# One kernel, its second mixer rewritten: projection in three parts, attention among the slabs, a new recurrent pipeline

## The chip, the cores and the metric

The program runs on one core of one Trainium2 chip. The metric is the device time of one execution in microseconds (us), so lower is better. A run of the kernel before takes 3675.67 us (median of three, 3661.73 to 3676.49). About 0.5% is what a measurement of this kernel can tell from no change.

## What is computed

Two transformer-like blocks of depth 2 follow each other over 512 positions of width 1024, all in float32. The change touches one mixer: the second layer of the first block. Cut to what matters there:

```python
h  = rms_norm(x, mix_norm[1])
p  = h @ w_in                                  # 1024 -> 2560 = 1024 (xb) + 1024 (gate) + 512 (mq)
xb, gate, mq = split(p, [1024, 2048])
xc = centred_depthwise_conv(xb, conv_w, conv_b)         # 4 taps along the positions
y  = rg_lru(xc, ..., False) + rg_lru(xc, ..., True)     # forward and backward
y  = y * gelu(gate)
mo = memory_attention(mq, mk, mv)              # 4 heads of 128, 256 memory rows, softmax
x  = x + concat([y, mo]) @ w_out[1]            # 1536 -> 1024
# rg_lru, for each block n of 128 channels (8 of them):
r = sigmoid(xc_n @ wa_n + ba);  i = sigmoid(xc_n @ wx_n + bx)
log_a = -8 * r * softplus(-lam);  a = exp(log_a)
u = sqrt(-expm1(2 * log_a)) * (i * xc_n);  h_t = a_t * h_(t-1) + u_t
```

## The kernel before

Activations are held transposed: 128 features on the partitions, 512 positions along the row, so a 1024-wide tensor is eight tiles of 128x512. A dense product reads its weights as *slabs* of 16 blocks of 128x128 (1 MB): SP loads a slab into `w_raw`, ScalarE (ACT) rounds it to `w_hi`, VectorE (DVE) makes the rest `w_lo`, and TensorE (PE) adds three products, hi·hi, hi·lo and lo·hi, per block (`TERMS`). Each of the three buffers holds two slabs, number s in half s % 2; the split of slab s+2 therefore waits until PE has finished slab s. `PHASES` lists the dense products in program order, and every engine walks through that list in its own instruction stream. Each stream is in order and is held up by semaphore waits that are written out by hand. There is no scheduler.

The second mixer is four stages, one after the other:

1. `in1_1` (`product`, PE line 764; `scaled`, DVE line 1367): ten slabs, each gives two tiles of `proj`. PE streams and the other engines split weights and evict.
2. `attention(SECTIONS["mem1"])`: four units of 128 positions. PE makes the scores (line 828), DVE copies and takes the maximum (1491, 1493), ACT the exponentials (1124), PE transposes (837), ACT copies (1138), PE weighs the values (847), DVE divides (1522), PE transposes back (859), DVE splits into `mixM_hi` and `mixM_lo` (1551, 1553).
3. `gates` (`lru_gates` on PE, `lru` on ACT and DVE, `gelu_arguments` on POOL): eight tiles. For each one DVE makes the convolution (1650), ACT and DVE its hi and lo parts (1167, 1662), PE four products in three terms each (907), ACT tanh and exp of them (1178, 1183, 1188, 1192), DVE the decays (1671 to 1678), ACT a square root (1197), DVE the two scans and the output (1686 to 1694), ACT and DVE `mixL_hi` and `mixL_lo` (1214, 1712).
4. `out1_1` (`product` again): eight slabs of 12 blocks, one output tile each. It starts with this wait, so all eight recurrent tiles come first:

```python
elif p.layer == 1:
    pe.wait_ge(y_ready, DT)
```

The activation tables of ACT have to be loaded anew between tanh or exp and the square root (`ACT_TABLE_LOAD`).

## Time and profile before

| | us |
|---|---|
| median of three runs | 3675.67 |
| the profiled execution, its own time | 3670.74 |
| its span, first to last instruction | 3668.9 |
| outside of the span | 1.8 |
| PE busy | 3364.1 (92%) |
| DVE busy | 1849.5 (50%) |
| ACT busy | 1120.0 (31%) |
| POOL busy | 460.1 (13%) |

PE is the busiest engine. Its matmuls are pipelined and overlap in the record, so a busy PE may still be slower than it could be. The span has three regions where PE is clearly less busy. The first of them is the second mixer, between 745.7 us and 1098.8 us; the rest of the program isn't touched by the change.

### The profile page before, as it was taken

What the parts mean: (1) busy time and instruction counts of PE and PEld (TensorE: products, weight loads), DVE (VectorE), ACT (ScalarE), POOL (GpSimd) and SP (SyncE); (2) the same over time, 40 slices, a digit from 0 to 9 for tenths busy, and PEclk for the clock granted to TensorE, in tenths of its full rate; (3) what the DMA queues carried; (4) which work ended last, traced back from release to release, by engine and by line L of the source; (5) the groups of instructions that cost most, each with busy time, mean ns of one, the idle gap of its engine ahead of it and who ended that gap; (6) DMA issues with size and microseconds to landing.
All of it is one profiled execution on the core that took longest, in us unless ns stands there. A gap on an engine that the chain in (4) does not pass through costs nothing.

```text
span 3668.9 us, 41039 instructions
## 1 busy us (share of the span) xinstructions
PE 3364.1 (92%) x15236; PEld 2759.4 (75%) x15236; DVE 1849.5 (50%) x1904; ACT 1120.0 (31%) x1267; POOL 460.1 (13%) x426
## 2 busy tenths in 40 slices
PE   8898999997379999999997689999999997689998
PEld 6687888885268887888885668888888885668886
DVE  5665534434955254544535654445444535654444
ACT  3243322223732122322314323223322314323221
POOL 1000100100120006000202620002000202620002
PEclk9899999998589999999997689999999997589999
DMA  3111222221022222422220012223322320012222
GB/s 139 53 47 49 100 103 92 100 95 40 9 77 92 103 92 97 115 93 97 98 101 35 1 37 101 91 99 104 108 102 87 107 92 35 1 44 94 92 99 73
DMA packets 46038, 292.98 MB, mean 80 GB/s; under 512 B 5408, under 2 KB 5920, under 8 KB 18432
## 3 DMA queue, kind: packets, MB, share of 16 engines
q1 hardware_dynamic: 44496, 287.04, 22.3%
q0 software_dynamic: 1456, 4.79, 0.8%
q8 instruction: 55, 0.90, 0.1%
q14 instruction: 31, 0.25, 0.0%
HBM read 289.70 MB, written 2.10 MB: 80 GB/s over the span
## 4 chain that ended last, share of the span: by engine, by line
PE 84%; DVE 9%; POOL 3%; ACT 2%; issue 2%; DMA 0%; DVEq 0%; SPq 0%; POOLq 0%; ACTq 0%
PE ps L764 76%; POOL dec L695 2%; PE ps L847 2%; PE ps L828 1%; PE ps L837 1%; DVE gfin L1806 1%; PE ps L796 1%; DVE mx L1493 1%; DVE xc L1650 1%; PE ps L807 1%; PE ps L966 1%; DVE w_lo L1319 0%; DVE sc_n L1488 0%; PE ps L859 0%; DVE tmp L1531 0%
## 5 line engine op out<-in xcount | busy, mean ns | idle before, releaser
L764 PE MATMUL ps<-xg_hi,w_hi 128*128 128x512 f32 x2592 | 1014.3, 391 | 17.6 <-DVE w_lo L1319 17.6
L764 PE MATMUL ps<-xg_lo,w_hi 128*128 128x512 f32 x2592 | 1009.5, 389 | 0.0
L764 PE MATMUL ps<-xg_hi,w_lo 128*128 128x512 f32 x2592 | 1009.2, 389 | 0.0
L1319 DVE TENSOR_TENSOR w_lo<-w_raw,w_hi 128x2048 fp32r<-128x2048 f32 (+1 forms) x292 | 681.6, 2334 | 280.0 <-ACT w_hi L1031 279.9
L1031 ACT ACTIVATE w_hi<-w_raw 128x2048 fp32r<-128x2048 f32 (+1 forms) x292 | 552.0, 1890 | 701.8 <-PE ps L764 701.8
L764 PEld LDWEIGHTS ps<-xg_hi,w_hi 128*128 128x128 f32 x2592 | 487.2, 188 | 121.6 <-issue 20.2
L764 PEld LDWEIGHTS ps<-xg_lo,w_hi 128*128 128x128 f32 x2592 | 487.2, 188 | 103.5 <-issue 2.7
L764 PEld LDWEIGHTS ps<-xg_hi,w_lo 128*128 128x128 f32 x2592 | 487.2, 188 | 101.2
L764 PE MATMUL ps<-hid_hi,w_hi 128*128 128x512 f32 x1216 | 473.4, 389 | 0.0
L764 PE MATMUL ps<-hid_lo,w_hi 128*128 128x512 f32 x1216 | 473.0, 389 | 0.0
L764 PE MATMUL ps<-hid_hi,w_lo 128*128 128x512 f32 x1216 | 473.0, 389 | 0.0
L1406 DVE SCALAR_TENSOR_TENSOR x<-ps,x 128x512 f32 (+1 forms) x128 | 88.6, 692 | 432.1 <-PE ps L764 432.1
L1394 DVE TENSOR_TENSOR tmp<-ps,r_bc 128x512 f32<-128x512 f32 x176 | 121.7, 692 | 323.2 <-PE ps L764 307.9
L764 PEld LDWEIGHTS ps<-hid_hi,w_hi 128*128 128x128 f32 x1216 | 228.2, 188 | 48.8 <-issue 1.4
L764 PEld LDWEIGHTS ps<-hid_hi,w_lo 128*128 128x128 f32 x1216 | 228.2, 188 | 47.5
L764 PEld LDWEIGHTS ps<-hid_lo,w_hi 128*128 128x128 f32 x1216 | 228.2, 188 | 47.0
L574 POOL TENSOR_TENSOR ssq<-x 128x512 f32<-128x512 f32 x9 | 9.3, 1038 | 1919.4 <-DVE x L1406 1919.4
L1084 ACT ACTIVATE xg_hi<-x,vec x72 | 52.1, 724 | 403.0 <-DVE x L1406 403.0
L1074 ACT ACTIVATE hid_hi<-tmp 128x512 f32 x88 | 55.7, 633 | 387.9 <-DVE tmp L1397 387.9
L1367 DVE TENSOR_TENSOR proj<-ps,r_bc 128x512 f32 (+1 forms) x76 | 52.5, 691 | 201.3 <-PE ps L764 200.9
L1072 ACT ACTIVATE tmp<-tmp 128x512 f32<-128x512 f32 x88 | 55.6, 632 | 269.0 <-DVE tmp L1394 269.0
L953 PE MATMUL ps<-fac 64*128 64x128 f32 (+1 forms) x576 | 82.6, 409 | 39.1 <-DVE fac L1755 38.0
(281 smaller groups left out, 3410.7 us busy)
## 6 DMA issues: line engine op xcount, KB each, us to landing
w_raw<-up_dram SPq DMA_DIRECT2D x120, 1024.0 KB, 4.7
w_raw<-in_dram SPq DMA_DIRECT2D x42, 1024.0 KB, 4.8
w_raw<-down_dram SPq DMA_DIRECT2D x32, 1024.0 KB, 4.7
w_raw<-down_dram SPq DMA_DIRECT2D x32, 768.0 KB, 4.2
w_raw<-down_dram SPq DMA_DIRECT2D x32, 640.0 KB, 3.9
w_raw<-out_dram SPq DMA_DIRECT2D x16, 768.0 KB, 4.2
w_raw<-out_dram SPq DMA_DIRECT2D x8, 1024.0 KB, 4.7
w_raw<-memk_dram SPq DMA_DIRECT2D x4, 1024.0 KB, 4.7
```

Of the source, the lines that this page charges most:

```text
L695: last = pool.tensor_tensor(to[:, :, u, :], (half, mid)[1 - u], (mid, half)[1 - u], ALU.subtract)
L764: last = pe.matmul(ps[:, 2 * q + b, :], (w_hi, w_lo)[wp][:, q, t:t + P], parts[xp], start=(k == 0 and m == 0), stop=(k == p.ktiles - 1 and ...
L847: last = pe.matmul(ps[:, u.o_bank, i * u.d:(i + 1) * u.d], turned(u)[:, kb, i * P:(i + 1) * P], u.v[kb][i], start=(kb == 0), stop=(kb == u ...
L953: last = pe.matmul(ps[:, 4 * (j % 2) + hd, c0:c0 + w], keys[:, s0:s0 + P], queries[:, t0:t0 + w], start=True, stop=True)
L1031: act.activation(w_hi[:, q, 0:w], w_raw[:, q, 0:w], ACT.Copy).then_inc(hi_done, 1)
L1072: act.activation(tmp[:, 0, :], tmp[:, 0, :], ACT.Silu).then_inc(silu_done, 1)
L1074: act.activation(pick(hid_hi, j), tmp[:, 1, :], ACT.Copy).then_inc(hid_h, 1)
L1084: act.activation(pick(xg_hi, m), pick(x, m), ACT.Copy, scale=g).then_inc(xg_h, 1)
L1319: dve.tensor_tensor(w_lo[:, q, 0:w], w_raw[:, q, 0:w], w_hi[:, q, 0:w].bitcast(F32), ALU.subtract)\
L1367: dve.tensor_tensor(pick(proj, j), ps[:, 2 * q + b, :], r_bc[:], ALU.mult)\
L1394: dve.tensor_tensor(tmp[:, b, :], ps[:, 2 * q + b, :], r_bc[:], ALU.mult).then_inc(evac, Q // 2)
L1406: dve.scalar_tensor_tensor(out=pick(x, m), in0=ps[:, 2 * q + b, :], scalar=p.alpha, in1=pick(x, m), op0=ALU.mult, op1=ALU.add).then_inc(ev ...
```

## The change

The projection is three phases now: `in1_1q` (memory queries, 2 slabs), `in1_1x` (recurrent input, 4), `in1_1g` (gate, 4). `out1_1` is six slabs of 16 blocks: for each half of the output (four tiles) one slab for the memory part and two for the recurrent part. From `in1_1x` on, each engine runs one hand-written sequence, `mixer()` (on POOL `lru()`). In the kernel's numbering, "inner" is an input slab and "outer" a gate slab. The gate weights of the recurrence are no longer split: they are loaded as float32 (`wg_lru`) and each product is one float32 matmul in place of three. Some steps of a tile move from DVE to POOL (squares of the decays, the sum of the two scans, the last factors of the gelu), and the root is taken on `l_t`. Buffers are laid out anew, so that `xg_hi` and `xg_lo` stay alive during the mixer.

```diff
@@ plan
+            ph.append(Phase("in1_1q", "proj", 2, 16, 2, norm=norm, layer=1, tile0=16))
+            ph.append(Phase("in1_1x", "mixer", 4, 16, 2, norm=norm, layer=1, tile0=0))
+            ph.append(Phase("in1_1g", "mixer", 4, 16, 2, norm=norm, layer=1, tile0=8))
+            ph.append(Phase("out1_1", "mixer", 6, 16, 4, alpha=1.0, last=True, next_norm=norm + 1, layer=1))
@@ SP
+            if p.name == "in1_1x":
+                sp.wait_ge(o_psum, SECTIONS["window"][-1].n + 1)
+                sp.dma_start(wg_lru[0][:], a["gates"][0]).then_inc(wg_in[0], 16)
+            if p.name == "out1_1":
+                sp.wait_ge(o_psum, M1[-1].n + 1)
+                sp.dma_start(wg_lru[1][:], a["gates"][1]).then_inc(wg_in[1], 16)
@@ POOL, lru()
+            def decay_squares(n):
+                if n:
+                    pool.wait_ge(sqrt_in, n)
+                pool.wait_ge(te_e, 2 * (n + 1))
+                pool.tensor_tensor(l_w[:], l_e[:, n % 2], l_e[:, n % 2], ALU.mult).then_inc(a2_done, 1)
...
+            for n in range(DT):
+                if n + 1 < DT:
+                    gelu_argument(n + 1)
+                state_sum(n)
+                if n + 1 < DT:
+                    decay_squares(n + 1)
+                    gelu_gate(n + 1)
@@ PE, mixer()
+            def gates(n):
+                pe.wait_ge(wg_in[n // 4], 16)
+                pe.wait_ge(conv_done, n + 1)
...
+                    pe.wait_ge(gate_read, n)
                 for g in range(4):
                     t = ((n % 4) * 4 + g) * P
+                    last = pe.matmul(ps[:, 4 + g, :], wg_lru[n // 4][:, t:t + P], xc[:, n % 3, :], start=True, stop=True)
+            def out(h, part):
+                s = MIX_O + 3 * h + part
+                pe.wait_ge(lo_done, s + 1)
+                if part == 0:
+                    pe.wait_ge(evac, EV0 + Q * (MIX_O + 3 * h))
+                for b in range(4):
+                    for k in range(4):
+                        if part and not (h or b):
+                            pe.wait_ge(y_ready, 4 * (part - 1) + k + 1)
...
+            inner(0)
+            scores(M1[0]); scores(M1[1])
+            inner(1)
+            turn_probs(M1[0]); scores(M1[2]); weigh(M1[0]); turn_probs(M1[1]); scores(M1[3]); turn_out(M1[0])
+            inner(2)
+            weigh(M1[1]); turn_probs(M1[2]); turn_out(M1[1]); weigh(M1[2]); turn_probs(M1[3]); turn_out(M1[2]); weigh(M1[3])
+            inner(3)
+            turn_out(M1[3])
+            outer(0); gates(0); outer(1); gates(1); outer(2); gates(2); outer(3); gates(3)
+            out(0, 0); gates(4); gates(5); out(0, 1); gates(6); gates(7); out(0, 2)
+            out(1, 0); out(1, 1); out(1, 2)
@@ ACT, mixer()
+            splits = {0: MIX_G + 3, 1: MIX_O, 2: MIX_O + 1, 3: MIX_O + 2, 5: MIX_O + 3}
             for n in range(DT):
+                if n in splits:
+                    split(splits[n])
+                if n + 3 < DT:
+                    first_tap(n + 3)
                 if n + 1 < DT:
                     gates(n + 1)
+                    root(n + 1)
+                high(n)
@@ DVE, mixer()
+            front(M1[0], 0); front(M1[1], 1); inner(0); split(MIX_X + 2); conv(0); inner(1); split(MIX_X + 3)
+            front(M1[2], 2); back(M1[0]); front(M1[3], 3); finish(M1[0]); inner(2); back(M1[1]); split(MIX_G); conv(1)
+            back(M1[2]); finish(M1[1]); finish(M1[2]); back(M1[3]); conv(2); inner(3); split(MIX_G + 1); finish(M1[3])
+            outer(0); split(MIX_G + 2); inputs(0); decays(0)
...
+            def decays(n):
+                dve.wait_ge(a2_done, n + 1)
+                dve.wait_ge(te_done, n + 1)
+                dve.scalar_tensor_tensor(out=l_t[:, n % 2], in0=l_w[:], scalar=1.0, in1=l_t[:, n % 2], op0=ALU.add,
+                                         op1=ALU.mult).then_inc(sqrt_in, 1)
...
+            for n in range(DT):
+                recur(n)
+                if n < 3:
+                    outer(n + 1)
+                if n in splits:
+                    split(splits[n])
+                if n + 1 < DT:
+                    inputs(n + 1)
+                    decays(n + 1)
+                output(n)
+                if n + 3 < DT:
+                    conv(n + 3)
+                low(n)
+            split(MIX_O + 4)
+            for b in range(4):
+                add(0, b)
```

(Statements that stand on lines of their own in the source are joined with ";" in the lists of PE and DVE.)

The order of the instructions shows it at two places. First ACT, from the last slab of the projection to the first recurrent tile (`sc` or `sc_m` are the scores, `pt` or `pt_m` the turned ones, `xc` the first tap of the convolution, `w_hi` a slab's split, `l_t` the gate). Before:

```order
L1031 ACTIVATE w_hi<-w_raw 128x2048
L1053 REGISTER_ALU
L1053 COMPARE_AND_BRANCH
L1124 ACT_TABLE_LOAD
L1124 ACTIVATE sc,rowsum<-sc,nmx 128x256 x8
L1138 ACTIVATE pt<-ps 128x1024
L1124 ACTIVATE sc,rowsum<-sc,nmx 128x256 x4
L1138 ACTIVATE pt<-ps 128x1024
L1124 ACTIVATE sc,rowsum<-sc,nmx 128x256 x4
L1138 ACTIVATE pt<-ps 128x1024 x2
```

And in the changed kernel:

```order
L1264 ACTIVATE sc_m,rowsum<-sc_m,nmx 128x256 x8
L1309 ACTIVATE xc<-proj,vec 128x512 x2
L1275 ACTIVATE pt_m<-ps 128x1024
L1172 ACTIVATE w_hi<-w_raw 128x2048
L1264 ACTIVATE sc_m,rowsum<-sc_m,nmx 128x256 x4
L1275 ACTIVATE pt_m<-ps 128x1024
L1172 ACTIVATE w_hi<-w_raw 128x2048
L1264 ACTIVATE sc_m,rowsum<-sc_m,nmx 128x256 x4
L1275 ACTIVATE pt_m<-ps 128x1024 x2
L1309 ACTIVATE xc<-proj,vec 128x512
L1172 ACTIVATE w_hi<-w_raw 128x2048 x2
```

Weight splits now stand between the steps of the attention. Second DVE, one tile of the recurrence, from one output to the next. Before:

```order
L1694 SCALAR_TENSOR_TENSOR l_y<-l_y,tmp 128x512
L1662 TENSOR_TENSOR xc_lo<-xc,xc_hi 128x512
L1671 SCALAR_TENSOR_TENSOR l_v<-l_v,xc 128x512 x2
L1675 SCALAR_TENSOR_TENSOR l_e<-l_e,l_t 128x1024
L1677 TENSOR_SCALAR l_a<-l_e 128x1024
L1678 SCALAR_TENSOR_TENSOR l_w<-l_a,l_e 128x1024
L1712 TENSOR_TENSOR mixL_lo<-l_y,mixL_hi 128x512
L1650 SCALAR_TENSOR_TENSOR xc<-proj,vec,xc 128x511 x2
L1650 SCALAR_TENSOR_TENSOR xc<-proj,vec,xc 128x510
```

And in the changed kernel:

```order
L1870 SCALAR_TENSOR_TENSOR l_y<-l_y,l_v 128x512
L1832 SCALAR_TENSOR_TENSOR xc<-proj,vec,xc 128x511 x2
L1832 SCALAR_TENSOR_TENSOR xc<-proj,vec,xc 128x510
L1875 TENSOR_TENSOR mixL_lo<-l_y,mixL_hi 128x512
L1861 TENSOR_TENSOR l_v<-l_v,l_t 128x1024
L1862 SCALAR_TENSOR_TENSOR l_v<-l_e,l_v 128x512
L1863 SCALAR_TENSOR_TENSOR l_v<-l_e,l_v 128x512
L1817 TENSOR_TENSOR proj<-ps,r_bc 128x512 x2
L1486 TENSOR_TENSOR w_lo<-w_raw,w_hi 128x2048
L1845 SCALAR_TENSOR_TENSOR l_v<-l_v,xc 128x1024
L1853 SCALAR_TENSOR_TENSOR l_t<-l_w,l_t 128x1024
```

The tile has fewer vector steps of its own, and the evictions of a gate slab and the split of a weight slab stand in the middle of it.

## Rows read from the trace of the kernel before

**Rows 1.** The page, part 2: PE busy tenths in 40 slices of the span.
```profile
PE   8898999997379999999997689999999997689998
```
**Rows 2.** Windows, four stages: stretch, length, busy PE, PEld, DVE, ACT, POOL; PEclk, DMA.
```profile
745.70:856.40 110.70, 109.82 (x483) 90.24 (x481) 41.66 (x33) 21.31 (x13) 2.70 (x2) 1.00 0.26 93
856.40:891.70 35.30, 24.57 (x144) 20.52 (x144) 21.14 (x29) 15.80 (x40) 7.86 (x6) 0.87 0.07 23
891.70:1030.30 138.60, 39.56 (x96) 28.38 (x96) 115.67 (x130) 91.61 (x119) 20.39 (x18) 0.60 0.02 6
1030.30:1098.80 68.50, 68.45 (x290) 56.43 (x291) 28.62 (x23) 18.01 (x15) 17.28 (x13) 0.96 0.27 93
```
**Rows 3.** Waits from 856 to 1031 us: us in total, times, longest.
```profile
PE ps L907 <- DVE xc_lo L1662: 76.9, 7, 13.2
...
PE ps L764 <- DVE mixL_lo L1712: 20.9, 1, 20.9
```
**Rows 4.** Timeline, DVE: start, us, engine line op; second evictions of two neighbouring slabs.
```profile
757.77 0.69 DVE L1367 TENSOR_TENSOR proj<-ps,r_bc 128x512 f32 x1 [0.51 <-PE ps L764]
...
768.64 0.69 DVE L1367 TENSOR_TENSOR proj<-ps,r_bc 128x512 f32 x1 [4.75 <-PE ps L764]
```
**Rows 5.** Timeline, PE, in the attention.
```profile
869.70 2.05 PE L847 MATMUL ps<-mv,pt 128*128 128x128 f32 x16 [0.16 <-ACT pt L1138]
871.58 1.04 PE L837 MATMUL ps<-ident,sc 128*128 128x128 f32 x8
872.46 1.89 PE L828 MATMUL ps<-mk,proj 128*128 128x256 f32 x8
```
**Rows 6.** Timeline, PE: four float32 products 128x512, two records for each.
```profile
2134.35 3.60 PE L966 MATMUL ps<-att,vtok_g 128*128 128x512 f32 x8
```
**Rows 7.** Timeline, DVE: a split; a convolution twice; a 128x1024 step; a scan.
```profile
857.50 2.29 DVE L1319 TENSOR_TENSOR w_lo<-w_raw,w_hi 128x2048 fp32r<-128x2048 f32 x1 [1.13 <-ACT w_hi L1031]
...
913.39 2.32 DVE L1650 SCALAR_TENSOR_TENSOR xc<-proj,vec,xc 128x511 f32<-128x511 f32 x3 [1.83 <-ACT xc L1160]
...
928.25 3.51 DVE L1650 SCALAR_TENSOR_TENSOR xc<-proj,vec,xc 128x511 f32<-128x511 f32 x3 [1.31 <-ACT xc L1160]
931.68 1.22 DVE L1686 SCALAR_TENSOR_TENSOR l_v<-l_v,l_w 128x1024 f32<-128x1024 f32 x1
932.93 1.22 DVE L1687 TENSOR_TENSOR_SCAN l_h<-l_a,l_v 128x512 f32<-128x512 f32 x1
```
**Rows 8.** Timeline, ACT: one tile of the recurrence, from root to root.
```profile
942.41 1.06 ACT L1197 ACTIVATE l_w<-l_w 128x1024 f32<-128x1024 f32 x1 [3.12 <-DVE l_w L1678]
943.38 0.80 ACT L1160 ACTIVATE xc<-proj,vec 128x512 f32<-128x512 f32 x1
944.19 1.28 ACT L1178 ACT_TABLE_LOAD   x1
945.49 0.69 ACT L1178 ACTIVATE l_t<-ps,hb 128x512 f32<-128x512 f32 x1
...
947.94 1.52 ACT L1183 ACTIVATE l_e<-l_t,lam_s 128x512 f32<-128x512 f32 x2
...
950.92 0.61 ACT L1192 ACTIVATE l_y<-l_y 128x512 f32<-128x512 f32 x1
...
958.45 1.06 ACT L1197 ACTIVATE l_w<-l_w 128x1024 f32<-128x1024 f32 x1 [3.12 <-DVE l_w L1678]
```
**Rows 9.** Timeline, POOL: the three gelu steps of one tile.
```profile
927.03 1.04 POOL L669 TENSOR_TENSOR l_y<-proj 128x512 f32<-128x512 f32 x1 [62.35 <-DVE mixL_lo L1712]
928.15 0.62 POOL L671 TENSOR_SCALAR l_y<-l_y 128x512 f32<-128x512 f32 x1
928.85 1.57 POOL L673 TENSOR_TENSOR l_y<-l_y,proj 128x512 f32<-128x512 f32 x1
```
**Rows 10.** Timeline, PE: start of the output product, and its first matmul at full rate.
```profile
1030.35 0.79 PE L764 MATMUL ps<-mixL_hi,w_hi 128*128 128x512 f32 x1 [20.92 <-DVE mixL_lo L1712]
...
1036.03 0.39 PE L764 MATMUL ps<-mixL_lo,w_hi 128*128 128x512 f32 x1
```

More of the change, by code:

```diff
@@ L780, in product @@
                 first = 2
-            with pe.Fori(first, p.slabs // 2) as i:
-                slab(i, 0)
-                slab(i, 1)
+            if first < p.slabs // 2:
+                with pe.Fori(first, p.slabs // 2) as i:
+                    slab(i, 0)
+                    slab(i, 1)
         def memory_slab(n):
@@ new lines, in scores @@
+        def scores(u):
+            if u.n:
+                pe.wait_ge(s_read, u.n)
+            if u.kind == "memory" and u.layer == 0:
+                pe.wait_ge(evac, EV0 + Q * (MEM_SLAB + MEM_SLABS))
+            for i in range(4):
+                for bank, col, off, n in score_pieces(u, i):
+                    o, keys = ps[:, bank, col:col + n], u.k[i]
+                    if u.kind == "near":
+                        o = o.rearrange("p (r c) -> p r c", c=SLAB_C)
+                    else:
+                        keys = keys[:, off:off + n]
+                    last = pe.matmul(o, u.q[i], keys, start=True, stop=True)
+            last.then_inc(s_ready, 1)
@@ new lines, in turn_out @@
+        def turn_out(u):
+            if u.kind == "near":
+                pe.wait_ge(on_ready, u.nf + 1)
+            else:
+                pe.wait_ge(o_ready, u.n + 1)
+            if u.f:
+                pe.wait_ge(ot_ready, u.f)
+            for t in range(u.ntile):
+                last = pe.transpose(ps[:, u.ot_bank, u.ot_col + t * P:u.ot_col + (t + 1) * P],
+                                    tmp[:, u.f % 2, t * P:(t + 1) * P], ident[:])
+            last.then_inc(ot_psum, 1)
+        def attention(us):
@@ L990, in _ @@
                     attention(SECTIONS["window"])
[L991 to L994 removed]
+                elif p.layer >= 2:
                     l = p.layer - 2
@@ L1001, in _ @@
                     gla(l)
-            elif p.kind == "gates":
-                lru_gates(p)
+            elif p.kind == "mixer":
+                if p.name == "in1_1x":
+                    mixer()
             elif p.kind == "resid" and p.src == "mix":
@@ L1220, in gla_prep @@
+            for b in range(4):
+                next_high(1, b)
+            split(MIX_END + 1)
         def gla_prep(p, l):
@@ L1286, in _ @@
                 rms(p.norm)
-            if p.kind == "gates":
-                lru(p, p.next_tiles * P)
+            if p.kind == "mixer":
+                if p.name == "in1_1x":
+                    mixer()
                 continue
@@ new lines, in mixer @@
+            inner(3)
+            split(MIX_G + 1)
+            finish(M1[3])
+            outer(0)
+            split(MIX_G + 2)
+            inputs(0)
+            decays(0)
+            splits = {0: MIX_G + 3, 1: MIX_O, 2: MIX_O + 1, 3: MIX_O + 2, 5: MIX_O + 3}
+            for n in range(DT):
[11 more added lines that the diff above has]
+                low(n)
@@ L1718, in gla_prep @@
+            split(MIX_O + 4)
+            for b in range(4):
+                add(0, b)
+                if b:
+                    next_low(0, b - 1)
+            next_low(0, 3)
+            split(MIX_O + 5)
+            split(MIX_END)
+            for b in range(4):
+                add(1, b)
+                if b:
+                    next_low(1, b - 1)
+            next_low(1, 3)
+            split(MIX_END + 1)
         def gla_prep(l):
@@ L1843, in _ @@
                 rms(p.norm)
-            if p.kind == "gates":
-                lru(p, p.next_tiles * P)
+            if p.kind == "mixer":
+                if p.name == "in1_1x":
+                    mixer()
                 continue
```

627 lines of the change are left out of this document (357 added, 270 removed).

## The prediction, made before the changed kernel ran

> **What bounds the kernel now.** I read PE's row by slices first. Among digits of 8 and 9 stands 7, 3, 7 for the tenth to twelfth slice [rows 1]. The windows of the four stages come next [rows 2]. In the projection (110.7 us) and the output product (68.5 us) PE is busy all the time. In the attention (35.3 us) it is busy for 24.6, and in the recurrence (138.6 us) for 39.6, while DVE is busy for 115.7 of these. So two stages of 174 us belong to DVE, ACT and their hand-overs, and PE waits. The waits say the same: the gate products waited 76.9 us for `xc_lo`, the output product 20.9 us for the last `mixL_lo` [rows 3]. The whole mixer takes 353.1 us. Only this part can change; the rest of the program has the same instructions.
>
> **What the change moves.** I write the time from the start of the first query slab, 745.7 us, as t = 0. The mixer ends at t = 353.1 now. I follow each engine's new order with the durations of the rows.
>
> PE alone. A slab of 48 matmuls takes 10.9 us (768.64 - 757.77) [rows 4]. One attention unit takes about 1.9 for the scores, 0.9 for the turn and 1.9 for the values (starts 869.70, 871.58, 872.46) and some 0.5 to turn the output, so 5.2, four of them 20.8 [rows 5]. The gate product of a tile was 12 matmuls, a quarter of a slab's, so 2.7 us at full rate; now it is four float32 products. Four of these took 3.6 us [rows 6], so I take 3.5 with the overlap off: eight tiles cost 28 us instead of 22. The output product has 288 blocks' matmuls before and after (8 slabs of 12 blocks, 6 of 16), six slabs of 10.9. Together 10 x 10.9 + 1 + 20.8 + 28 + 65.2 = 224 us. Below that the mixer can't go.
>
> Part A, queries and inputs with the attention. Six slabs (65.2), the norm's sum (1), attention (20.8). The waits that remain for PE, each read from the orders: second scores behind the copy of the first, 1.3 (a 128x1024 step is 1.22 [rows 7]); fourth scores behind DVE's split, 1.9 (a split is 2.29 [rows 7]); two turns and one value product behind a split and a convolution on ACT and DVE, 0.4 + 1.7 + 2.7. Sum 8. Part A ends at t = 95. Splits hide behind PE's slabs, as they do in the projection now [rows 2].
>
> Part B, gate slabs with tiles 0 to 3. PE needs 10.9 + 3.5 per tile, so it could be through at 95 + 58 = 153. DVE can't follow. Its steps between the decays of one tile and of the next are: output and `mixL_lo`, 0.7 each; convolution, 2.3; product with the root and two scans, 3 x 1.22; inputs and decays, 2 x 1.25; two evictions, 1.4; one split, 2.3. Sum 13.5 [rows 4, 7]. On top comes POOL. While POOL's gelu steps run, the convolution takes 3.51 instead of 2.32 [rows 7, 9]. The POOL work beside it is about 0.5 of the short step and 1.26 to 1.57 of the last one, say 1.7 to 2.1, so DVE loses 0.6 to 0.7 us per us of POOL. POOL now has per tile the same three steps (2.9), a step of 128x1024 (twice 1.04), one more short step (0.6) and two more of 1.3 [rows 9], 8.2 us instead of 3. The square falls where DVE waits for it, so 6.1 of them meet DVE: 0.7 x 6.1 = 4.3. Period: 13.5 + 4.3 = 17.8.
> ACT's period, for comparison: tap and table load 2.1, from the first tanh to the end of the gelu's tanh 6.0, load 1.3, root 1.1, high part 0.6, split 1.9, thus 13 us [rows 8]. It waits for DVE, not the other way.
>
> The first tile is in step with PE: gate products of tile 0 end at 110; tanh, exp and square make the decays end at 117 (ACT 2.5 + 1.6, then POOL 2.1 and DVE 1.25). Tile 1's gates on ACT stand behind a split that needs PE's slab of t = 121, so its decays end at 133. Then the period rules: 151 and 169. The last gate slab is evicted after tile 2's scans, at 162. The first output slab waits for exactly this, so PE is idle from 153 to 162. After such a gap PE is slow: at the start of the output product it issued 13 matmuls in 5.7 us, 0.44 each instead of 0.23, before it was at full rate [rows 10], a loss of 2.6. The slab ends at 175.5.
>
> Part C, tiles 4 to 7. ACT has a split that needs this slab, ahead of tile 4's gates: 175.5 + 1.9 + 0.8 + 1.3, tanh 2.5, exp 1.6, square 2.1, decays 1.3, so 187. Then DVE's steps without evictions: 13.9 (no split) gives 201, 16.2 (with one) 217, and without a convolution 10.6 gives 228. From there the last tile needs root and high part of tile 6 (1.8), its low part 0.7, product and scans 3.7, POOL's sum 1.3, output 0.7, high 0.6, low 0.7, about 9.8: t = 238. The third output slab has been waiting for this with 39 of its 48 matmuls to go: 8.9 + 2.6 at the low rate, 249.
>
> Part D, the turn between the halves. The split of slab `MIX_O + 4` stands ahead of the four additions on DVE, and its high part waits for the slab that has just ended: 1.9 + 2.3. Then four additions and three low parts, 5 us. PE waits 9.3 us, which it never did in the output product before [rows 2]: 258.5. Three slabs and one slow start, 32.7 + 2.6: the mixer ends at t = 294.
>
> **Sum.** 353.1 - 294 = 59 us less. Against the profiled execution, 3668.9 in its span and 3670.74 in all, this gives 3612. That execution lies 5 us below the median of 3675.67 and inside its runs (3661.73 to 3676.49), so I keep the number and allow for the scatter in the range. The two loads of `wg_lru` (1 MB each) cost nothing: SP issues the first behind long finished work and the second behind the last value product, both some 15 us or more before their use, and the DMA share is 0.26 at most [rows 2]; if SP were held, PE would wait at tile 4 where it waits anyway.
>
> **The price I know least** is that of POOL beside DVE. Lower end: none, as if the steps didn't meet. Then the periods are 13.5, 9.9, 12.2, 7.6 and the same sum ends near 273 with no cold slabs counted, 80 us less: 3591. Upper end: every POOL us stops DVE for a us. That is 1.8 per tile more on six tiles, 11 us: 3623. I take 0.7, from the one row that shows it.
> The page "SBUF — State Buffer" of the Trainium skill (section "SBUF: two separate sides") says that GpSimd and a DVE step with two SBUF inputs take turns on one shared pair of ports, each for the whole instruction, and that the other is blocked fully; by that rule the upper end is right. The row [rows 7, 9] agrees in kind, the 1.2 us lost are somewhat under the 1.7 to 2.1 of POOL's work, so for now it stands for less than a full block. It is a rival below.
> The page "ScalarE: Activation LUTs" of the Trainium skill (section "What ACT_TABLE_LOAD costs") gives 1283 ns for a load and some 1380 ns more for a drain; here the tanh starts 1.30 us after its load (944.19, 945.49) [rows 8], so no drain of that size shows in front of it. By the page tiles 5 and 7 would wait for ACT and the sum would grow by about 3 us.
>
> **The rivals.**
> - *Light meeting.* DVE and POOL seldom meet, because DVE's evictions read PSUM and POOL has idle time between its waits. For it: POOL is busy 8 of 18 us only. Against it: most of its steps are released by DVE's own steps, so they start beside the next one. 3591.
> - *Full block*, as above: 3623. For it: a POOL step of 1.26 took 1.57 beside DVE [rows 9], so both lose. Against it: the missing 0.5 us or more in the row.
> - *PE sets the pace all through*, as the weave intends: 224 us for the mixer, 129 less, 3542. Against it: DVE's 13.5 per tile is already 93% of PE's 14.4 before any contention, and tiles 4 to 7 have two slabs to hide behind, not four.
> - *PE stays at the low clock* (the other side). In the recurrence PE's granted clock was 0.60 of full on average [rows 2], a mix of its two levels, 1.2 and 2.4 GHz, because each burst came after a gap of 11 us. In the new order PE has gaps of 4 to 10 us from t = 153 on. If these kept it low for all of its work from t = 110 on, 125 us, each matmul would take 0.43 to 0.44 instead of 0.23, some 110 us more: 3722. It decides from about 67 us of work at the low clock that I count at the high one; beyond 88 the kernel is slower by more than 0.5%. Against it: in the output product the rate was full after 5.7 us of work [rows 10], and the slabs here last 10.9 each.
> - *It does little*: the recurrent loop still takes 17 us per tile as before (958.45 - 942.41 = 16.0 [rows 8]) and nothing of the attention hides, because hand-overs that I count at nothing add up. Saved would be only the projection beside it, less than 18 us, about 3660. Against it: half of the tiles lie beside gate slabs that PE must do anyway.
>
> **How the numbers follow.** Forecast with 0.7: 56%, 3612, by itself 3602 to 3622. Light meeting 17%, full block 17%, PE's pace 3%, low clock 4%, little 3%. The likeliest gives the time, 3612. The range takes in both ends of the contention and about 8 us for hand-overs and the scatter of the runs: 3588 to 3634. Faster by over 0.5% (18 us) 0.93, within 0.5% 0.03, slower 0.04.
>
> **What the new profile would show.** PE's row of slices without a 3. The time from one 128x1024 root to the next about 18 us for tiles 1 to 3, then 14, 16, 11. Convolutions and scans beside POOL at 1.3 to 1.6 times their length. A wait of PE for the last gate eviction near 9 us, three waits in the third output slab for `mixL_lo` that add up to about 25, and one of 9 us for the additions. Float32 gate products at 0.9 us. A mixer of about 294 us. I am wrong if the mixer's length lies outside 270 to 316, or if these waits add up to under 20 us.

## The result, and the profile after

The changed kernel took 3634.74 us (median of 4 runs, 3633.96 to 3636.28), the kernel before in the same session 3676.08 (3661.73 to 3676.60). The ratio is 0.9894, with a 95% interval from 0.9882 to 0.9907: 41 us less, where 59 were forecast. The time lies 0.7 us above the upper end of the range.

The page, part 1 and the slices of part 2, of the kernel after:
```profile
PE 3375.8 (93%) x15204; PEld 2758.4 (76%) x15204; DVE 1832.8 (50%) x1852; ACT 1109.6 (31%) x1255; POOL 539.1 (15%) x458
...
PE   8898999999589999999996699999999997699998
```
The hole 7, 3, 7 in PE's row [rows 1] has become a single 5. PE works more closely in the mixer, and it still waits there.

To compare kernels whose lines have moved I measure the mixer between two instructions that neither kernel changes: the reciprocal of the norm ahead of it and that of the norm behind it. I call this the stretch. DVE's two reciprocals in the kernel after (start, us, engine, line, operation, idle before it and its releaser):
```profile
754.93 3.35 DVE L1590 RECIPROCAL r_bc<-r_bc 128x512 f32<-128x512 f32 x1 [1.01 <-ACT r_bc L1232]
...
1065.08 3.35 DVE L1590 RECIPROCAL r_bc<-r_bc 128x512 f32<-128x512 f32 x1 [4.00 <-ACT r_bc L1232]
```
The stretch is 310.15 us; before it was 352.74 (752.88 to 1105.62). It lost 42.6, not 59. The start of the first query slab, t = 0 of the prediction, is 747.7 in the kernel after.

Windows of the stretch before and after (length, then busy time of PE, PEld, DVE, ACT, POOL; PEclk, DMA):
```profile
752.88:1105.62 352.74, 242.05 (x1011) 195.25 (x1010) 207.01 (x213) 146.74 (x185) 48.24 (x39) 0.82 0.15 54
```
```profile
754.93:1065.08 310.15, 244.10 (x978) 184.85 (x977) 191.07 (x162) 136.04 (x173) 127.26 (x71) 0.88 0.17 61
```
DVE's busy time fell by 16 us and ACT's by 11. POOL's went from 48 to 127 us. Run alone, the moved steps are worth some 5.3 us per tile [rows 9], 42 in all (an estimate), which leaves 37 of the 79 more for steps that took longer beside DVE.

The four parts of the prediction as windows of the kernel after (they answer to [rows 2]): A to t = 100.4, B to the last gate slab's eviction, C to the end of the third output slab, D the second half.
```profile
747.70:848.10 100.40, 89.78 (x436) 74.35 (x435) 49.90 (x56) 28.35 (x49) 2.70 (x2) 0.97 0.18 63
848.10:914.60 66.50, 57.44 (x226) 41.91 (x225) 51.63 (x41) 45.55 (x53) 42.90 (x24) 0.95 0.22 79
914.60:1010.20 95.60, 60.42 (x176) 39.28 (x176) 69.78 (x49) 51.45 (x63) 62.72 (x33) 0.75 0.10 33
1010.20:1055.30 45.10, 36.26 (x149) 29.86 (x150) 17.81 (x18) 10.71 (x11) 15.09 (x12) 0.89 0.19 70
```
In part C PE is busy for 60 of 96 us, at a mean granted clock of 0.75: most of its idle time is there.

PE's waits after (timeline; compare [rows 3]; between these rows stand work and other waits, the longest of them 3.94 and 5.20 for ACT at the gate products of tiles 5 and 7):
```profile
790.43 0.80 PE L965 MATMUL ps<-xg_hi,w_hi 128*128 128x512 f32 x1 [3.97 <-DVE proj L1817]
...
914.60 0.76 PE L1012 MATMUL ps<-mixM_hi,w_hi 128*128 128x512 f32 x1 [9.06 <-DVE proj L1817]
...
977.00 0.79 PE L1012 MATMUL ps<-mixL_hi,w_hi 128*128 128x512 f32 x1 [5.78 <-DVE mixL_lo L1875]
...
991.45 0.80 PE L1012 MATMUL ps<-mixL_hi,w_hi 128*128 128x512 f32 x1 [12.80 <-DVE mixL_lo L1875]
...
998.48 0.80 PE L1012 MATMUL ps<-mixL_hi,w_hi 128*128 128x512 f32 x1 [5.38 <-DVE mixL_lo L1875]
...
1019.04 0.77 PE L1012 MATMUL ps<-mixM_hi,w_hi 128*128 128x512 f32 x1 [8.85 <-DVE x L1881]
```
The forecast waits are there at their size: 9.06 for the last gate eviction (9), 5.78 + 12.80 + 5.38 = 24.0 in the third output slab (25), 8.85 for the additions (9.3). The first row was not forecast, nor were the two waits for ACT.

Decays of tiles 0 to 7 (DVE L1853) end at t = 122.1, 138.4, 156.4, 174.4, 192.0, 208.2, 226.2 and 240.6. The periods, each from one tile's decays to the next, are 16.3, 18.0, 18.0, 17.6, 16.2, 18.0 and 14.4 for tiles 1 to 7.

### The profile page after: what moved, and what is told of

Its sections match the earlier page's. It is cut to its first block, busy times and chain, and to the rows that moved or that the text cites. A ratio compares the mean times of both kernels' runs of the same rounds, so it can differ in the third digit from the quotient of the medians.

```text
span 3633.5 us, 40771 instructions
## 1 busy us (share of the span) xinstructions
PE 3375.8 (93%) x15204; PEld 2758.4 (76%) x15204; DVE 1832.8 (50%) x1852; ACT 1109.6 (31%) x1255; POOL 539.1 (15%) x458
## 4 chain that ended last, share of the span: by engine, by line
PE 84%; DVE 7%; POOL 4%; ACT 2%; issue 2%; DMA 0%; DVEq 0%; POOLq 0%; SPq 0%; ACTq 0%
PE ps L823 73%; POOL dec L754 3%; PE ps L906 2%; PE ps L965 2%; PE ps L887 1%; PE ps L1012 1%; PE ps L896 1%; DVE gfin L2034 1%; PE ps L856 1%; PE ps L867 1%; DVE mx L1659 1%; PE ps L1112 1%; DVE w_lo L1486 1%; POOL l_v L719 0%; POOL l_w L707 0%
## 5 line engine op out<-in xcount | busy, mean ns | idle before, releaser
L823 PE MATMUL ps<-xg_hi,w_hi 128*128 128x512 f32 x2464 | 964.3, 391 | 17.6 <-DVE w_lo L1486 17.6
L823 PE MATMUL ps<-xg_lo,w_hi 128*128 128x512 f32 x2464 | 959.5, 389 | 0.0
L823 PE MATMUL ps<-xg_hi,w_lo 128*128 128x512 f32 x2464 | 959.3, 389 | 0.0
L823 PEld LDWEIGHTS ps<-xg_hi,w_hi 128*128 128x128 f32 x2464 | 463.2, 188 | 116.2 <-issue 20.3
L823 PEld LDWEIGHTS ps<-xg_lo,w_hi 128*128 128x128 f32 x2464 | 463.2, 188 | 98.3 <-issue 2.7
L823 PEld LDWEIGHTS ps<-xg_hi,w_lo 128*128 128x128 f32 x2464 | 463.1, 188 | 96.5
L1534 DVE TENSOR_TENSOR proj<-ps,r_bc 128x512 f32 (+1 forms) x60 | 41.4, 691 | 152.7 <-PE ps L823 152.4
```

The costliest lines, as they stand in the source:

```text
L823: last = pe.matmul(ps[:, 2 * q + b, :], (w_hi, w_lo)[wp][:, q, t:t + P], parts[xp], start=(k == 0 and m == 0), stop=(k == p.ktiles - 1 and ...
```

## The experiments

All in us. The times of the first two rows and of the last four are medians of four runs, the others single runs. A stretch is from one profile of each kernel. How well it repeats can be read where kernels share their order up to the last tile: there the decays of tile 7 end 233.4 or 233.5 behind the first reciprocal (after, narrow sums, own banks, interleaved). The whole time scatters more, because parts outside the mixer do, so I compare stretches.

| kernel | stretch | time |
|---|---|---|
| before | 352.7 | 3676.08 |
| after | 310.2 | 3634.74 |
| gate slabs ahead of the tiles | 333.8 | 3652.95 |
| attention ahead of the inputs | 310.0 | 3635.45 |
| output slabs behind the last gates | 310.1 | 3630.07 |
| output slabs behind the last tile | 330.7 | 3654.00 |
| first inner slab evicted first | 303.5 | 3631.80 |
| narrow POOL steps | 289.4 | 3607.53 |
| POOL's square first | 310.1 | 3635.43 |
| square of the decays on ACT | 299.4 | 3618.79 |
| gate products half as wide | 306.4 | 3624.85 |
| last sums of squares narrow | 306.7 | 3628.82 |
| own banks for the second half | 297.6 | 3623.53 |
| and the halves interleaved | 283.0 | 3611.11 |
| the three best together | 272.2 | 3597.10 |
| and four squares of the next norm on ACT | 267.0 | 3588.27 |

**Which part of the change gains what.** Four runs undo three parts, the last part in two steps. The lists of ACT and DVE follow PE's new order in each; the code shown is PE's, cut.

Gate slabs ahead of the recurrent tiles:
```
             outer(0)
-            gates(0)
             outer(1)
-            gates(1)
             outer(2)
-            gates(2)
             outer(3)
+            gates(0)
+            gates(1)
+            gates(2)
             gates(3)
```


> Undoes another part: all gate slabs of the second mixer run ahead of its recurrent tiles instead of among them; all else as in the changed kernel. A (the weave of gate slabs and tiles is what lets VectorE and GpSimd begin the tiles while TensorE works, and it is the greater part of the 42.5 gained): the stretch is 15 to 35 longer than 310.2, so 325 to 345. B (the gain is from the output halves and the attention): 310 to 316. In A the scans beside GpSimd keep their length (1.5 to 2.0 against 1.2 alone), since the same instructions meet.


Measured: 23.7 longer, 333.8. This weave is the larger half of the gain (A). DVE's decays of tiles 2 and 3, which have no evictions and no split beside them here:
```profile
931.24 1.62 DVE L1856 SCALAR_TENSOR_TENSOR l_t<-l_w,l_t 128x1024 f32<-128x1024 f32 x1 [3.01 <-POOL l_w L707]
...
947.19 1.62 DVE L1856 SCALAR_TENSOR_TENSOR l_t<-l_w,l_t 128x1024 f32<-128x1024 f32 x1 [3.00 <-POOL l_w L707]
```
Their periods are 15.9, for 18.0 with the gate slabs, and DVE waits 3.0 in each for POOL's square, for 0 with them. The new steps of a tile were not undone by a run, but these 15.9 stand beside the 16.0 of a tile before [rows 8]: DVE's steps became fewer, and the tile hardly shorter.

Memory attention ahead of the input slabs, which then alternate between two pairs of banks:
```
+            scores(M1[0]) ... turn_out(M1[3])
             inner(0)
-            scores(M1[0]) ...
             inner(1)
```


> Undoes one part: the memory attention runs behind the query slabs and ahead of the input slabs, all else as in the changed kernel. In the kernel before, the attention stage took TensorE 35.3 for 20.8 of its own work; woven among the slabs TensorE waits 10.6 in sum up to the end of the inputs. A (the weave hides the attention's waits, 14.5 becomes 10.6, and the tiles begin as much later as the inputs do): the stretch is 4 to 9 longer than 310.2, so 314 to 319. B (the attention hides nothing that counts, because tiles and slabs behind it are paced by VectorE from the mixer's inputs on, and the inputs are ready as early): within 2 of 310.2. C (the whole 14.5 comes back on top): 323 to 326.


Measured: 0.1 shorter (B). As it stands, the weave of the attention gains nothing: DVE's product of tile 0 (L1861) comes 115.6 after the reciprocal, 116.2 in the changed kernel. Why is seen below, at the wait that was not forecast.

Output slabs behind the last tile's gate products:
```
-            out(0, 0)
             gates(4)
             gates(5)
-            out(0, 1)
             gates(6)
             gates(7)
+            out(0, 0)
+            out(0, 1)
```


> Undoes a third part: the first two slabs of the output product run behind the last tile's gate products instead of among tiles 4 to 7; their splits on ScalarE and VectorE stand where they stood, but for the last two, which move behind the tiles. All else is as in the changed kernel (stretch 310.2). A (the output weave hides what it holds): two slabs, 21.8, and the 39 of 48 matmuls that the third still had to do turn into three whole slabs and a slow start behind the last tile, 35.3 for 11.8, less some 2 that the tiles gain because no gate product stands behind a slab: the stretch is 326 to 334. B (the slabs among tiles 4 to 7 hold the tiles up by as much as they hide): 308 to 318.


Measured: 310.1, as B has it, but B's reason is only a small part of it. The last gate products end at 963 in this run, some 30 us ahead of the last `mixL_lo` (992.71). Both slabs found room in that gap and ended at 985: that is where A's reckoning was wrong. The last tile ended 3.9 us earlier than in the changed kernel (239.6 for 243.5 behind the reciprocal), and PE lost it again, since the third slab waited for its split, which now stands behind the tiles, and had all of its 48 matmuls to go. The last four periods are 15.9, 15.9, 16.0 and 14.5. Tiles 4 and 6 lost 1.7 and 2.0, with the two splits that moved; tiles 5 and 7, which had none, stayed within 0.3. DVE waited 3.0 for POOL in each of the four. So PE's slabs in front of the gates don't make tiles 5 and 7 slow; for tile 6 the run doesn't tell slab and split apart.

One wait more, so that the slabs begin where they did before the change:
```
+                if (h, part) == (0, 0):
+                    pe.wait_ge(y_ready, DT)
```


> The kernel of the last run with one wait more: TensorE begins the first output slab only when the last tile's mixed low half is there, as the output product of the kernel before did. (In the last run, with the slabs behind the last gate products, the stretch was still 310.1: the last gate products end a tile and a half before the last tile does, and two slabs found room in that gap.) A (the room beneath the last tiles is the second part of what the change gains): two slabs of 10.9 come back whole, less the third slab's own wait of 2.6 for its split, so the stretch is 327 to 333. B (the output product's place is worth nothing, as the last run might be read): 308 to 314.


Measured: 330.7, 20.6 longer than without that wait, the last run (A). PE in this run, at the first output slab:
```profile
993.99 0.77 PE L1014 MATMUL ps<-mixM_hi,w_hi 128*128 128x512 f32 x1 [28.23 <-DVE mixL_lo L1879]
```
So 23.7 is from gate slabs beside tiles 0 to 3 and about 20.6 from two output slabs beneath the last tiles. Together that is 44.3 for the 42.6 gained; I did not undo both in one kernel, so that the two add up is not shown.

**The wait that was not forecast.** `inner(0)` and `inner(1)` use the same two banks, and DVE evicts `inner(0)` behind the fronts of two attention units. Moved ahead of them:
```
+            inner(0)
             front(M1[0])
             front(M1[1])
-            inner(0)
```


> Mixer stretch = from the start of the reciprocal of the norm ahead of the mixer to the one behind it; 352.7 us in the kernel before, 310.2 in the changed one. Here DVE evicts input slab 0 ahead of the first two attention units. Theory A (the input slabs share one pair of PSUM banks, so the second one waits for an eviction that stands behind both units on DVE: 3.97 us idle): the wait falls under 1.5 us, the second scores wait some 1.3 us longer, gate slab 0 starts 2 to 4 us earlier, and the stretch is 2 to 4 us shorter, 306 to 308. Rival B (the time before the recurrence doesn't matter, because DVE sets the end): the stretch stays at 310.


Measured: 6.6 shorter, more than A's 2 to 4. The wait is gone, and the second scores wait 1.32 as before. PE at `inner(1)` in the changed kernel, and then in this run:
```profile
790.43 0.80 PE L965 MATMUL ps<-xg_hi,w_hi 128*128 128x512 f32 x1 [3.97 <-DVE proj L1817]
791.02 0.63 PE L965 MATMUL ps<-xg_lo,w_hi 128*128 128x512 f32 x1
...
795.29 0.60 PE L965 MATMUL ps<-xg_hi,w_lo 128*128 128x512 f32 x1
795.72 0.41 PE L965 MATMUL ps<-xg_hi,w_hi 128*128 128x512 f32 x1
```
```profile
789.24 0.58 PE L965 MATMUL ps<-xg_hi,w_hi 128*128 128x512 f32 x1
789.65 0.40 PE L965 MATMUL ps<-xg_lo,w_hi 128*128 128x512 f32 x1
...
792.19 0.39 PE L965 MATMUL ps<-xg_hi,w_hi 128*128 128x512 f32 x1
```
With the wait, the slab's first 12 matmuls start 0.43 apart, but for 0.59 behind the first, and take 5.29 us (790.43 to 795.72). Without it they take 2.95 (789.24 to 792.19). Windows of the changed kernel give the granted clock (the figure behind POOL's): 0.50 for these 12, 1.00 right behind them.
```profile
790.43:795.72 5.29, 5.29 (x13) 4.13 (x13) 4.31 (x4) 2.27 (x6) 0.00 (x0) 0.50 0.35 116
795.72:801.20 5.48, 5.48 (x26) 4.53 (x25) 0.69 (x1) 0.00 (x0) 0.00 (x0) 1.00 0.20 82
```
So the wait costs its 4.0 and 2.3 more in matmuls at the lower of PE's two clock levels. Here also is why the attention's weave gained nothing: in the run with the attention apart there is no such wait. With the eviction moved, the weave is worth 6.5 (310.0 to 303.5).

**POOL and DVE.** The gelu steps and the sum of both directions work on 64 instead of 512 columns from tile 2 on; the other columns of these results are not computed. The square keeps its size.
```
+                c = S if n < 2 else 64
-                g, y = proj[:, 8 + n, :], l_y[:, n % 2, :]
+                g, y = proj[:, 8 + n, 0:c], l_y[:, n % 2, 0:c]
```


> From tile 2 on, POOL's gelu steps, gelu factors and sums of the two scans work on 64 of 512 columns (the rest of each tile isn't computed); the squares of the decays stay whole. That takes some 5 us of POOL work per tile away. Theory A (a POOL step and a DVE step with two SBUF inputs take turns, and what POOL works DVE loses): DVE's steps return to their lengths without POOL (scan 1.2, split 2.3), the decays of tiles 1 to 7 come 13 to 15 us apart instead of 14.5 to 18, and the stretch is 14 to 24 us shorter, 286 to 296. Rival B (the loss is in hand-overs and PE's low clock): at most 5 us shorter, 305 or more.


Measured: 289.4, 20.8 shorter (A), though the periods are not the 13 to 15 that A gives. Those of tiles 5, 6 and 7 are 11.6, 13.6 and 10.4, so 4.6, 4.4 and 4.0 less than after. DVE's waits for the square in them fell too, from 3.03, 1.78 and 3.00 to 2.07, 1.79 and 2.06, so 1.9 of the 13.0 is waits and 11.1 is DVE's steps. The period of tile 4 rose from 17.6 to 19.6: DVE waits there 2.48 and 3.01 for ACT, whose split needs PE's slab. How the two engines meet, DVE and POOL in tile 4 of the changed kernel:
```profile
944.41 1.22 DVE L1861 TENSOR_TENSOR l_v<-l_v,l_t 128x1024 f32<-128x1024 f32 x1
945.66 1.94 DVE L1862 TENSOR_TENSOR_SCAN l_v<-l_e,l_v 128x512 f32<-128x512 f32 x1
947.52 1.56 DVE L1863 TENSOR_TENSOR_SCAN l_v<-l_e,l_v 128x512 f32<-128x512 f32 x1
949.01 2.25 DVE L1845 SCALAR_TENSOR_TENSOR l_v<-l_v,xc 128x1024 f32<-128x1024 f32 x1
```
```profile
944.63 1.89 POOL L696 TENSOR_TENSOR l_y<-proj 128x512 f32<-128x512 f32 x1 [2.08 <-DVE mixL_lo L1875]
946.61 1.41 POOL L698 TENSOR_SCALAR l_y<-l_y 128x512 f32<-128x512 f32 x1
948.10 2.07 POOL L700 TENSOR_TENSOR l_y<-l_y,proj 128x512 f32<-128x512 f32 x1
```
Read the ends. DVE's product ends at 945.63, POOL's step 0.89 later (946.52), DVE's scan 1.08 later (947.60), POOL's next 0.42 later (948.02), the second scan 1.06 later (949.08). In these rows the engines alternate: each instruction is recorded as started, and ends about its own time (1.04 and 0.62 for POOL's two [rows 9], 1.22 for a scan) behind the end of the other engine's. The narrow POOL steps show it from the other side:
```profile
962.92 1.14 POOL L697 TENSOR_TENSOR l_y<-proj 128x64 f32<-128x64 f32 x1 [2.30 <-DVE mixL_lo L1878]
...
976.73 0.32 POOL L722 TENSOR_TENSOR l_v<-l_v 128x64 f32<-128x64 f32 x1 [5.74 <-DVE l_v L1866]
```
A 128x64 step takes 0.32 alone and 1.14 where DVE is at work. The page "SBUF — State Buffer" of the Trainium skill (section "SBUF: two separate sides") gives a lock for the whole instruction and a loser that is fully blocked. The trace agrees, by the ends above. That my factor of 0.7 is an average over a convolution that met POOL in part would fit this, but no run shows it.

POOL squares the decays ahead of its sum of both directions:
```
+                    decay_squares(n + 1)
                     state_sum(n)
-                    decay_squares(n + 1)
```


> POOL squares the decays of tile n+1 ahead of the sum of tile n's scans instead of behind it. Theory A (the queue on POOL is late for DVE's decays in tiles 4 to 7, waits of 1.8, 3.0, 1.8 and 3.0 us for the square): each of the four waits falls by 1 to 2 us and the stretch is 4 to 7 us shorter, 303 to 306. Rival B (POOL's order doesn't matter, its total does): the output waits for the sum instead, the stretch stays within 1 us of 310.


Measured: 310.1 (B). DVE's waits for the square fell from 3.03, 1.78 and 3.00 to 1.79, 0 and 1.78 in tiles 5 to 7, but its step for the decays rose from 1.62 to 2.30, 2.28 and 2.27, since the sum now lies beside it. The same work in another order moves the meeting and doesn't remove it.

ACT squares the decays:
```
-                pool.tensor_tensor(l_w[:], l_e[:, n % 2], l_e[:, n % 2], ALU.mult).then_inc(a2_done, 1)
+                act.activation(l_w[:], l_e[:, h], ACT.Square).then_inc(a2_done, 1)
```


> ACT squares the decays (one activation of 128x1024, some 1.06 us) instead of POOL (1.89 us alone, up to 3.95 beside DVE). Theory A (POOL's work stops DVE, us for us): 1.9 us less per tile where DVE is never idle (tiles 1 to 3) and 1 to 3 us less where it waited for the square, together 10 to 16 us: 294 to 300. Rival B (a square that falls where DVE waits costs only its own length, as the prediction had it): 0.8 us per tile, 304 or more. Rival C (ACT is then late): no gain.


Measured: 299.4, 10.7 shorter (A, at its upper edge). DVE's decays of tiles 5 to 7 in the changed kernel, and in this run:
```profile
954.28 1.62 DVE L1853 SCALAR_TENSOR_TENSOR l_t<-l_w,l_t 128x1024 f32<-128x1024 f32 x1 [3.03 <-POOL l_w L707]
...
972.24 1.62 DVE L1853 SCALAR_TENSOR_TENSOR l_t<-l_w,l_t 128x1024 f32<-128x1024 f32 x1 [1.78 <-POOL l_w L707]
...
986.68 1.62 DVE L1853 SCALAR_TENSOR_TENSOR l_t<-l_w,l_t 128x1024 f32<-128x1024 f32 x1 [3.00 <-POOL l_w L707]
```
```profile
949.34 2.30 DVE L1848 SCALAR_TENSOR_TENSOR l_t<-l_w,l_t 128x1024 f32<-128x1024 f32 x1
...
966.35 1.62 DVE L1848 SCALAR_TENSOR_TENSOR l_t<-l_w,l_t 128x1024 f32<-128x1024 f32 x1
...
978.15 1.86 DVE L1848 SCALAR_TENSOR_TENSOR l_t<-l_w,l_t 128x1024 f32<-128x1024 f32 x1 [0.35 <-ACT l_w L1327]
```
The waits are all but gone and the periods are 13.8, 16.3 and 12.0, against 13.9, 16.2 and 10.6 of the prediction. These three tiles give 6.5 of the 10.7. Tiles 2 and 3, where DVE didn't wait, became 1.5 and 0.6 shorter: the square had met DVE there, at less than its own length of 1.89.

**PE's own work.** Gate products over 256 of 512 columns; the rest of the gates is left out.
```
-                    last = pe.matmul(ps[:, 4 + g, :], ..., xc[:, n % 3, :], ...)
+                    last = pe.matmul(ps[:, 4 + g, 0:256], ..., xc[:, n % 3, 0:256], ...)
```


> The float32 gate products cover 256 of 512 columns (the other half isn't computed): 14 us of PE less. Theory A (DVE sets the pace, PE is not on the path in the recurrence): the first tile comes 1.7 us earlier, and the stretch is at most 4 us shorter. Rival B (PE's float32 gates cost their length): 10 us or more shorter.


Measured: 3.8 shorter (A). Half of 28 us of PE work gives 3.8 back, and the first tile comes 1.5 earlier: PE does not set the pace. (The periods stayed as they were.)

**The tail.** POOL's last four squares and sums for the next norm on 64 columns, the rest left out:
```
+                c = S if m < 4 else 64
+                pool.tensor_tensor(sq[:, 0:c], x[:, m, 0:c], x[:, m, 0:c], ALU.mult)
```


> POOL's sums of squares for the last four tiles of the next norm cover 64 of 512 columns (the rest isn't computed). Theory A (the four tiles come 2.7 us apart now instead of 8.2, POOL needs 2.8 to 4.5 for each, and the norm's product waited 2.35 us behind them): the time from the last addition to the reciprocal falls from 9.8 to under 7 us, and the stretch is 3 us shorter, 307. Rival B (the norm waits for PE's slab, not for POOL): unchanged.


Measured: 3.5 shorter (A); from the end of the last addition to the reciprocal it is 6.3 instead of 9.8. In the changed kernel PE waits at the end for POOL's sum:
```profile
1062.25 2.07 PE L791 MATMUL ps<-ssq,ones 128*128 128x512 f32 x2 [2.35 <-POOL ssq L606]
```

**Versions.** The second output half in banks 4 to 7, the banks of the gate products; its first slab waits until ACT has read the last of these:
```
-                            last = pe.matmul(ps[:, b, :], ...
+                            last = pe.matmul(ps[:, 4 * h + b, :], ...
```


> The second half of the output product sums in PSUM banks 4 to 7, so it needs no addition of the first half. Theory A (PE's 8.85 us wait for the additions, and the slow matmuls behind it, are on the path): the wait goes to 0, and the stretch is 8.9 + up to 2.6 us shorter, 299 to 302. Rival B (the wait moves to the next split, which stands behind the same slab): 306 or more.


Measured: 12.6 shorter, 1.1 more than A's most; ratio to before 0.9865 (0.9845 to 0.9884). PE's wait of 8.85 for the additions is gone, and the slow matmuls behind it; from the last addition to the reciprocal it is 9.6 instead of 10.5.

Then the slabs of both halves in the order M, L0, M, L0, L1, L1:
```
+    OUT_AT = {(0, 0): 0, (0, 1): 1, (1, 0): 2, (1, 1): 3, (0, 2): 4, (1, 2): 5}
```


> As the last one, and the slabs are taken in the order memory, tiles 0 to 3 for both halves, then tiles 4 to 7 for both, so PE does two more slabs while the last tiles are on their way. Theory A (PE idles 24 us in the third output slab for tiles 5 to 7, and the end is the last tile plus what is left for PE): after the last tile some 9 + 11 us are left instead of 57, and the stretch is 30 to 38 us shorter, 272 to 280. Rival B (the two slabs and their splits delay DVE's tiles, and the gain is half): 290.


Measured: another 14.6 shorter, 283.0; ratio 0.983 (0.981 to 0.985). That lies between A and B, and neither has the reason. The tiles were not delayed (tile 7's decays end at 233.5 for 233.4), so B's is wrong. A left out that the second half shares the gates' banks: its first slab can't start until the last gates are read. In place of the three waits of 24.0 there is one, for these:
```profile
978.95 0.76 PE L1015 MATMUL ps<-mixM_hi,w_hi 128*128 128x512 f32 x1 [9.57 <-ACT l_v L1323]
```
Behind it PE has four slabs to do, and 25 us of them lie behind the last `mixL_lo` (999.36), where A counted 20.

The last two runs add up what helped: the interleaved order, the early eviction and the square on ACT.


> Three edits together on the changed kernel: layer 0 of the second output half woven ahead of layer 1 of the first (with banks of its own), the first inner slab evicted ahead of the two fronts, and the squares of the decays on ScalarE. The stretch from the reciprocal of the norm ahead of the second mixer to that of the norm behind it is 310.2 in the changed kernel (352.7 before). A (what ends the stretch is the meeting of VectorE and GpSimd in tiles 4 to 7 plus slabs that wait for mixed halves): the three gains are partly the same idle time of TensorE, so the stretch is 265 to 280, the time 3590 to 3604. B (each edit has its own wait, they add up): 250 to 262, the time 3575 to 3588. C (the interleave alone already took all of it): stretch as in the interleaved kernel alone, time 3607 or more.


Measured: 272.2 (A); ratio 0.9786 (0.977 to 0.9802). The three edits gave 27.2, 6.6 and 10.7 in kernels of their own, 44.5 in sum, and 38.0 together.
The last one also takes four squares of the next norm off POOL:
```
+                act.activation(tmp[:, m % 2, :], x[:, m, :], ACT.Square).then_inc(sq_done, 1)
```


> The kernel of the run beside it, and the squares for the following norm of tiles 4 to 7 move from GpSimd to ScalarE; GpSimd only adds them. A (GpSimd's sums for the next norm stand late behind the last tiles): 2 to 4 less than the run beside it. B (the end is TensorE's slabs and VectorE's additions): no difference above 1. C (ScalarE's squares stand ahead of the tanh or exp of the next stage, or its additions are as long as its products): up to 2 more.


Measured: 267.0, 5.2 less than the run beside it (A, and more than its 4); ratio 0.9764 (0.9748 to 0.978), 3588.27 us. This version beats both kernels.
```profile
754.88:1021.85 266.97, 235.49 (x979) 181.04 (x978) 187.55 (x162) 145.42 (x185) 99.20 (x59) 0.95 0.19 67
```
PE is busy for 235 of 267 us; the prediction's floor for PE was 224.

## Why the prediction was right in kind and 23 us too low

The direction, PE's waits and the periods of tiles 2 and 3 came out. The mixer ended at t = 307 (1054.57, the last addition), so inside the 270 to 316 that the prediction set as its test; the forecast was 294. Of the 23 us, 16.4 are in the stretch (59 forecast, 42.6 gained), and they stand at three steps. Some 7 more are outside the mixer.

*Part A: "Sum 8. Part A ends at t = 95."* It ended at 100.4. The listed waits were there (1.32, 1.99, 0.27, 1.64, 1.44, so 6.7 for 8). Missing was PE's wait for a bank, 3.97, and the 2.3 of slow matmuls behind it. I had followed data and not banks. The eviction moved ahead gave back 6.6. Missed: 5.4.

*Part B* held in its numbers: the period was 18.0 for 17.8, and the first decays came at 122 for 117, shifted by part A alone. In part this is luck. The square was counted as falling where DVE waits, but in tiles 2 and 3 DVE didn't wait, so all 8.2 us of POOL's steps ran beside a busy DVE and not 6.1; the loss was still 4.5 (18.0 - 13.5), for 4.3.

*Part C: "Then DVE's steps without evictions: 13.9 gives 201, 16.2 gives 217, and 10.6 gives 228."* The periods were 16.2, 18.0 and 14.4. The failed step is an earlier sentence: "The square falls where DVE waits for it, so 6.1 of them meet DVE". It took the square out of the meeting and then put the wait nowhere. While gate slabs last, evictions and splits fill that place, and the wait is 0 in tiles 2 and 3. Behind them it stands open: 3.03 + 1.78 + 3.00 = 7.8 us. The run with the gate slabs ahead shows the same wait, 3.0, in tiles 2 and 3. The square on ACT removed the waits and brought the three periods to 42.1 in sum, where the prediction had 40.7. The price of the meeting was not what failed. The three measured periods are 48.6 in sum: 29.7 of DVE's own steps (the 9.9, 12.2 and 7.6 of the prediction's lower end), 11.1 that the narrow POOL steps gave back apart from waits, and 7.8 of waits. (With the narrow steps they are 35.6, which is 29.7 and 5.9 of waits.) The prediction had 29.7, 11.0 and nothing. Missed with tile 4: 7.4.

That the waits in the third output slab came out at 24.0 for 25 is luck in part. By the forecast (end at 249, 25 of waits, 13.5 of work) PE begins this slab at t = 210.5. It began at 222.3 (969.97). Of these 11.8, 5.4 are part A's. The rest came with waits of 3.94 and 5.20 for ACT that no term has, and the gate products behind the two took 5.4 and 6.6 us and not 3.6.

*Part D: "Three slabs and one slow start: the mixer ends at t = 294."* The wait for the additions was 8.85 for 9.3. But the four last tiles of `x` come 1.3 to 2.7 us apart, and POOL takes 2.8 to 4.5 for the square and sum of each, so its sums pile up behind the last one. From the start of the last addition to the reciprocal there are 10.5 us (1054.57 to 1065.08), before there were 6.9 (1098.72 to 1105.62). Missed: 3.6.

The three sum to 16.4.

*The base: "so I keep the number".* I took the profiled execution, 3670.74, and not the median of 3675.67. Two stretches with the same instructions in both kernels differ between the profiles. The second one before, and after:
```profile
1823.30:2199.93 376.63, 308.87 (x1483) 251.46 (x1482) 200.70 (x213) 109.24 (x146) 102.19 (x111) 0.84 0.13 45
```
```profile
1781.99:2164.36 382.37, 317.31 (x1483) 258.38 (x1482) 200.68 (x212) 109.45 (x146) 102.08 (x111) 0.81 0.13 44
```
With the same 1483 matmuls the stretch is 5.7 us longer, at a granted clock of 0.81 instead of 0.84. The first stretch of the program is the other (370.7 and 373.4). Over all kernels here, whose code is the same there, these two took 370.7 to 373.7 (once 376.4) and 375.4 to 382.6. So the profile fell by 35.4 only, the medians by 41.3. What decides which length a kernel gets was not tried, and stays open.

*The rivals.* "Light meeting" is refuted: the narrow POOL steps gave 20.8. "Full block" was right in its mechanism, as the ends of the instructions show. Its price was 1.8 per tile over mine, 5.4 on tiles 5 to 7; without the waits the narrow steps gave 11.1 there, where I had 11.0. So the mechanism is the rival's and the price is nearer mine: the 3623 of the rival was nearer to the result than 3612, but not for its reason. "PE sets the pace" is refuted by the narrow gates. "PE stays at the low clock" is refuted: the two slabs whose starts I followed (790.43 and 1019.04) had 12 slow matmuls of 48 each, and the stretch has a mean granted clock of 0.88. "It does little" is refuted by the gate slabs.

Two slips change nothing: the DMA share is 0.27 at most and not 0.26 [rows 2], and when I add up the light meeting again from its own periods I get about 268 for the 273 stated.

The page "ScalarE: Activation LUTs" of the Trainium skill (section "What ACT_TABLE_LOAD costs") adds a drain to each load. ACT in tile 6 of the kernel after:
```profile
958.18 1.89 ACT L1172 ACTIVATE w_hi<-w_raw 128x2048 fp32r<-128x2048 f32 x1
960.09 1.28 ACT L1320 ACT_TABLE_LOAD   x1
961.38 0.69 ACT L1320 ACTIVATE l_t<-ps,hb 128x512 f32<-128x512 f32 x1
```
The load starts 0.02 us behind the end of the split, and the tanh 1.29 us after the load's start, so the trace shows no drain of that size on either side.

## What to carry to other kernels

When an order of work is forecast, follow each engine for three things: data, buffers, and the step for which it waits. The two largest errors here were a bank that was not followed and a wait that was taken out of one term and put in no other. A wait that other work hides in one phase must be priced again where that work ends. Undoing one part shows what it is worth in its place only: the attention's weave was worth nothing until one eviction moved, and 6.5 us then.

## What the runs showed of the hardware

A wait of PE of 3.97 us cost 2.3 more in matmuls at a granted clock of 0.50; behind one of 1.99 (811.32) the next slab's matmuls start 0.23 apart (814.31, 814.54). Where they met, DVE and POOL took turns, instruction by instruction: a POOL step of 0.32 us lasted 1.14, a scan of 1.22 lasted 1.94. Moving POOL's square ahead of its sum left the stretch as it was (310.1 for 310.15); taking the square to ACT (299.4) or making other steps smaller (289.4) helped. Four float32 products of 128x512 took 3.6 us at the high clock (873.29), 0.9 each, as forecast, and 5.4 to 6.6 behind waits. Stretches with the same code differed by up to 7 us from one kernel to another (375.4 to 382.6), and the longer had the lower granted clock in the pair shown (0.81 and 0.84).
